# Three table rows taken out of the first loads, their spacing made 4/3 slots, and a gate step placed earlier on ScalarE

## The reference

```python
c_act = silu(c)
mod = c_act @ mod_w[l] + mod_b[l]                  # 6 vectors of 1024: sh1, sc1, g1, sh2, sc2, g2
h = rmsnorm(x, norm_g[l, 0]) * (1 + sc1) + sh1
proj = h @ w_in; q, k, v, og, gl = split(proj)
log_a = log_sigmoid(gl @ w_g2 + b_g2) / 16
b = cumsum(log_a)                                  # within chunks of 64 tokens
q_t = q * exp(b); k_t = k * exp(-b); k_dec = k * exp(b_last - b)
o = ...                                            # scores, values and a state carried over 4 chunks
x = x + g1 * ((rmsnorm(o, norm_g) * silu(og)) @ w_out)
cos, sin = rope_tables(positions)                  # needed much later, in the second block
```

## Time and profile before

| what | us |
|---|---|
| median of 3 runs | 3123.09 |
| lowest and highest | 3121.48, 3126.27 |
| profiled execution, its own time | 3126.55 |
| its span, first to last instruction | 3124.7 |
| first 16 modulation rows and norm, until TensorE starts slot 16 | 53.19 |
| slots 16 to 40 | 94.7 |
| from there to the start of slot 41 | 34.1 |

### The profile page before, as it was taken

One profiled execution on the slowest core, in us unless ns is written; L12 is line 12 of the kernel. 1 busy time (PEld: TensorE's weight loads), 2 busy tenths in 40 slices (PEclk: granted clock), 3 DMA queues, 4 the chain that ended last, 5 costly groups with the idle time before them and its releaser, 6 DMA issues.

```text
span 3124.7 us, 58935 instructions
## 1 busy us (share of the span) xinstructions
PE 2964.2 (95%) x18896; PEld 2681.5 (86%) x18896; DVE 2061.9 (66%) x3764; ACT 1578.5 (51%) x3099; POOL 1338.2 (43%) x1069
## 2 busy tenths in 40 slices
PE   7999999988999988999999799999899999999998
PEld 6679999987787777899999677878898889999997
DVE  6647953368888866389213988888653447777776
ACT  1225554577455555355555964555564235555554
POOL 5823988886544410069888844444000010000100
PEclk8999999999999997999999999999999999999998
DMA  6534557722766631445567046665354235555553
GB/s 248 206 105 153 182 194 263 262 106 76 260 229 225 221 120 55 138 158 183 180 214 259 0 179 249 226 221 206 129 179 139 95 128 193 191 194 197 193 192 124
DMA packets 153463, 552.58 MB, mean 177 GB/s; under 512 B 16896, under 2 KB 19712, under 8 KB 153232
## 3 DMA queue, kind: packets, MB, share of 16 engines
q1 hardware_dynamic: 151136, 547.42, 51.3%
q10 hardware_dynamic: 2224, 3.87, 0.4%
HBM read 550.17 MB, written 1.05 MB: 176 GB/s over the span
## 4 chain that ended last, share of the span: by engine, by line
PE 79%; ACT 8%; DVE 5%; issue 5%; POOL 3%; DMA 1%; ACTq 0%; DVEq 0%; POOLq 0%; SPq 0%
PE bank L983 20%; PE bank L1013 20%; PE bank L1256 12%; PE bank L724 7%; PE bank L776 7%; PE bank L1277 6%; ACT hT L1485 3%; POOL w_parts L2580 2%; PE bank L748 1%; ACT hT L1481 1%; PE bank L678 1%; ACT h_parts L1493 1%; DVE a_parts L2216 1%; DVE h_parts L2213 1%; ACT h_parts L1491 1%
## 5 line engine op out<-in xcount | busy, mean ns | idle before, releaser
L2580 POOL TENSOR_TENSOR w_parts<-ring,w_parts 128x512 fp32r<-128x512 f32 x512 | 659.3, 1307 | 423.4 <-ACT w_parts L1445 400.6
L983 PE MATMUL bank<-h_parts,w_parts 128*128 128x256 f32 x6144 | 750.1, 284 | 6.0 <-ACT arena L1381 4.4
L983 PEld LDWEIGHTS bank<-h_parts,w_parts 128*128 128x128 f32 x6144 | 741.7, 192 | 6.8 <-issue 4.8
L1445 ACT ACTIVATE w_parts<-ring 128x512 fp32r<-128x512 f32 x512 | 319.5, 631 | 342.6 <-PE bank L983 241.7
L1256 PEld LDWEIGHTS bank<-h_parts,w_parts 128*128 128x128 f32 x3072 | 374.5, 193 | 3.9 <-DVE arena L2442 1.5
L1256 PE MATMUL bank<-h_parts,w_parts 128*128 128x256 f32 x3072 | 375.4, 284 | 1.4 <-DVE arena L2442 1.4
L1643 ACT ACTIVATE w_parts<-ring 128x512 fp32r<-128x512 f32 x384 | 242.2, 632 | 266.2 <-PE bank L1256 166.1
L1013 PE MATMUL bank<-h_parts,a_parts 128*128 128x512 f32 x1536 | 366.4, 394 | 8.3 <-DVE a_parts L2216 8.3
L1013 PE MATMUL bank<-w_parts,a_parts 128*128 128x512 f32 x1536 | 371.6, 398 | 0.6 <-DVE a_parts L2216 0.6
L2511 DVE TENSOR_TENSOR w_parts<-ring,w_parts 128x512 fp32r<-128x512 f32 x376 | 271.0, 732 | 148.9 <-ACT w_parts L1643 145.7
L1013 PEld LDWEIGHTS bank<-h_parts,a_parts 128*128 128x128 f32 x1536 | 284.3, 188 | 84.5 <-DVE a_parts L2216 26.4
(11 more groups left out here) (345 smaller groups left out, 4492.2 us busy)
## 6 DMA issues: line engine op xcount, KB each, us to landing
ring<-stream SPq DMA_DIRECT2D x786, 512.0 KB, 3.4
arena<-stream SPq DMA_DIRECT2D x144, 512.0 KB, 4.3
hT<-stream SPq DMA_DIRECT2D x80, 512.0 KB, 4.5
mean<-stream SPq DMA_DIRECT2D x32, 512.0 KB, 4.5
arena<-consts ACTq DMA_DIRECT2D x1, 1536.0 KB, 6.6
xT<-xin ACTq DMA_DIRECT2D x1, 1024.0 KB, 10.8
out<-hT SPq DMA_DIRECT2D x4, 256.0 KB, 2.2
arena<-subk ACTq DMA_DIRECT2D x2, 128.0 KB, 2.1
```

The lines of the kernel that those rows point to most:

```text
L983: mm = pe.matmul(bank[k][:, 0:T], w[:, wp, ws], h_parts[:, hp, 4 * j + q, :], start=(j == 0 and q == 0 and i == 0), stop=(j == 1 and q == ...
L1445: act.activation(w_parts[half % HALVES][:, 0, :], ring[slot_][:, j * 512:(j + 1) * 512], ACT.Copy).then_inc(sem(f"{n}_high"), 1)
L2580: pool.tensor_tensor(w[:, 1, :], ring[(base + k) % RING][:, j * 512:(j + 1) * 512], w[:, 0, :].bitcast(F32), ALU.subtract).then_inc(sem(f" ...
```

## The change

The list `at` begins at slot 17 in place of slot 8, has 20 entries spaced by 4/3 slots in place of 14 spaced by 3/2, and leaves four in place of six behind slot 43. ScalarE's sigmoid and logarithm stand behind the eviction of the first key tile instead of the fourth.

```diff
             gla = MO["gla_gl"][0]
-            at = [8, 10, 14, gla + 1] + [gla + 2 + 3 * i // 2 for i in range(14)] + [gla + 27] * 6
+            at = [gla + 1 + 4 * i // 3 for i in range(20)] + [gla + 27] * 4
             loads_with_mods(0, MO["peer0_q"][1], MODS_GLA, MODS_GLA[0], at)
...
             for h in range(GH):
                 copy_act(act, G.q[:, h, :], f"g_q{h}")
-            for h in range(GH):
-                copy_act(act, G.k[:, h, :], f"g_k{h}")
-
+            copy_act(act, G.k[:, 0, :], "g_k0")
             act.wait_ge(sem("g_abs"), 1)
             act.activation(G.e, G.e, ACT.Sigmoid, scale=-1.0).then_inc(signal("g_act"), 1)
             act.wait_ge(sem("g_act"), signalled("g_act"))
             act.activation(G.e, G.e, ACT.Ln).then_inc(signal("g_ln"), 1)
             act.wait_ge(sem("g_ln"), signalled("g_ln"))
+            for h in range(1, GH):
+                copy_act(act, G.k[:, h, :], f"g_k{h}")
```

## The result

The changed kernel takes 3137.73 us, median of 20 runs (3119.06 to 3149.29), against 3124.44 (3114.95 to 3131.55, 20 runs) for the kernel before, measured with it: ratio 1.0038, 95% interval 1.0023 to 1.0052. It is slower, by 13 us, where 5 were forecast; 3137.73 lies above the range of 3117 to 3133.

A forecast was written before the change was run, and what follows sets the result against it. It took VectorE's first rows, then TensorE, with POOL's table rows just beginning to bind, as the bound. The 8.7 us won was nearly all lost to the rope, and late POOL rows made slot 40 5 later: 3123.1 + 5 = 3128, range 3117 to 3133.

The forecast's parts named there:

- Part 1: Start of the kernel: with rows moved out of the first loads, slot 16 starts at about 44.5, 8.7 us earlier.
- and still do: Start of the kernel: TensorE's last two direct rows run 31.45 to 38.44 as before, their loads waiting for the same readers.
- Part 2: VectorE's rope beside busy POOL: done at 65.3, slot 20 stalls 6.4; of the 8.7 us won, 0.6 is left.
- Part 3: POOL's table rows fall behind: row 6 starts at 82.9, so rows 6 to 15 must be made from there on.
- Part 4: Gate step three slots earlier: no gain itself; its chain costs POOL 16.6 us, all ahead of row 15, 2.8 previously behind it.
- The sum: Row 15 made at 144.5, slot 40 ends at 153 against 147.85, slot 41 due at 187: 5 us later, 3128.
- rival (b): Start's gain kept, POOL makes its 16 rows by 131: 3115 us; against it, rows need 88 and 82 are there; chance 0.12.
- 34.1 us of mostly TensorE work lead to 181.99: Stretch from slot 40's end at 147.85 to TensorE's start on slot 41, read from the profile before.
- Rival (c): No gap in POOL's first rows: rope ends at 68, late slots bring a second low-clock spell; 3132 us; chance 0.25.

The follow-up runs named there:

- e3: The changed kernel with ScalarE's two sines moved behind the key evictions and VectorE's sign product behind the gate chain; 3130.56 us, ratio 1.002.
- e2: The changed kernel with the old list of places put back, so only the gate's step is moved early; 3123.75 us, ratio 1.0004.
- e1: The kernel before with only the new list of places, the gate step left where it was; 3131.13 us, ratio 1.0029.
- e6: The kernel before with 30 tiny logarithms on ScalarE ahead of the head norms' logarithms, to make slot 41 late; 3129.64 us, ratio 1.001.
- a5: The changed kernel, unaltered, one profiled run; 3130.72 us at a clock of 0.974.
- a4: The changed kernel, unaltered, one profiled run; 3144.53 us at a clock of 0.969.
- a1: The changed kernel, unaltered, run again; 3129.19 us over 12 runs, ratio 1.0027.
- x3: The changed kernel with the table rows behind slots 38 and 39 moved to slot 41; 3139.93 us over 6 runs, ratio 1.005.
- z1: x3 with VectorE's two output-gate scalings moved behind the first four state copies; 3129.13 us over 9 runs, ratio 1.0027.
- e7: The changed kernel with late sines, respaced table rows and the last modulation group taken behind slots 41 to 48; 3123.64 us, ratio 0.9994.
- z2: e7 with VectorE's two output-gate scalings moved behind the first four state copies; 3108.48 us over 6 runs, ratio 0.9962.
- x2: e7, unaltered, one profiled run; 3119.53 us.
- x4: The kernel before with three table rows put behind slot 39, so that slot 40 waits long; 3140.91 us over 6 runs, ratio 1.0047.

## Why the prediction was wrong, point by point

- **Part 1 held, the gain is larger.** Slot 16 starts at 41.93, forecast 44.5. The last two direct rows run from 29.05 instead of 31.45, 2.4 of the 2.6: "and still do" was wrong. The load they wait for is issued 0.4 earlier (25.74 against 26.16) and lands after 3.3 instead of 5.3. It no longer has POOL's rows beside it on the queue, which is the likely reason; no run tests it. The gain is worth nothing, as the rope takes it.
- **Part 2 held.** The rope begins at 43.90 (46.4) and ends at 64.27 (65.3), 1.07 an operation, slot 20 starts at 65.78 (66.7) behind 7.91 (6.4). e3 shows that this wait is the reason: with the sines out of the way slot 41 is 8 earlier in the profile.
- **Part 3 held.** Row 6 starts at 82.23 (82.9).
- **Part 4: the price on POOL held, its cause in the move didn't.** Rows 6 to 15 take 82.23 to 143.65, 61.4, so the chain costs 16.4 beside ten rows of 4.5 (forecast 16.6, of which 0.86 was a wait of POOL for a load, at 102.25 in before). But that the move itself costs 2.8 was not borne out: e2 has row 15 only 1.1 later and slot 41 not later at all. With the new list the chain lies ahead of row 15's end at either place, since POOL is late there: e1, with the gate late, needs the same 61.4 for rows 6 to 15.
- **The sum held for the lower heap.** Row 15 is made at 143.65 (144.5), slot 40 ends at 152.5 (153), slot 41 starts at 186.63 (187). The lower heap's median is 5.2 over before, inside the range, and e6 shows that a slot 41 as late as this costs 4.7. One figure of rival (b), "82 are there", doesn't follow from its own numbers: from 43.8 to 131 are 87.2.
- **The term that failed is "34.1 us of mostly TensorE work lead to 181.99".** It was taken as a constant behind slot 40, and what POOL does there was costed only by its last row. It measured 34.1 again in the profiles of after (152.5 to 186.63) and a5, and 47.6 in a4 (151.9 to 199.51), which has the spell. The step that makes the difference had a row of its own in the trace of before, L1970 at 1.88 beside a POOL that had just paused. After the change POOL pauses at most 1.5 near there instead of 7.2, and in which of its four operations the scalings fall depends on when its last loads land. Where they fall on the product and first fold they take 3.1 to 3.7, TensorE waits half a microsecond or more, and in part of the runs its clock then goes to 1.2 GHz for most of the stage: 14 us. Eleven of the 20 runs lie in the upper heap, so the median stands there. How many do varies: a1, the same kernel, had 4 of 12 and a median of 3129.19, inside the range. So it is partly chance that the median of 20 came out at 3137.73. None of the rivals had this. Rival (c) had a second spell of low clock, but behind the stalls of the late slots, at 1.7 apiece.

Shown: the spell costs 14.0 (a4 against a5); it comes without a late stall (x3); with the wait taken away it is gone from the trace, and the clock is higher in each run, in the kernel whose runs all had a low clock (x3 against z1), and the upper heap of e7 is empty (z2). Not shown: the upper heap of after has one trace, a4; its other runs are known by their time and clock alone, and x2 shows that these don't settle it. Why a wait of 0.5 to 0.6 goes with the spell in two profiles of six is open, and so are e3's runs at 3130 to 3134, the three runs of e1 over 3140 and the one of e2: their kernels' profiles have no wait, but each is of a faster run. The edit of z1 on the changed kernel as it stands was not tried; by z1 one would expect it to leave the lower heap alone, some 5 over before.

## What to carry to other kernels

When work is shifted in time on one engine, look not only at who waits for it, but at which operations of another engine it now meets, above all ahead of a stage that TensorE runs alone with narrow products: in this kernel a wait of half a microsecond there went with a loss of 14 in some runs. An operation that nobody needs yet should not stand ahead of one that TensorE waits for. And when the runs of a kernel fall into two heaps, take traces until there is one of each, and compare those.

## What the runs showed of the hardware

- TensorE's granted clock fell to 0.50 in the state stage in four profiles, each with a wait of TensorE of 0.50 to 1.07 us ahead. In x2, x3 and x4 it fell within half a microsecond of the wait's end, in a4 2.6 behind it. It stayed there for 27 us in a4 (163.5 to 190.8) and 34 in x3 (157.0 to 191.2), although the engine was busy 5.00 of each 5 us. The products in it were of 64 columns, with groups of eight of 256 columns in between; such a group (L893) took 3.78 instead of 1.99. In each the clock rose again only while TensorE ran the 16 products of 256 columns behind them (L900).
- The same wait doesn't always go with it: 0.49 (twice), 0.55 and 0.63 brought no spell; 0.50, 0.54, 0.87 and 1.07 did.
- Two scalings of 128x1024 on VectorE take 1.6 (a1) to 3.7 us (x3, z1), by what POOL runs beside them.
- VectorE's 19 rope operations took 20.4 us beside a busy POOL (after) and 10.0 where POOL paused for most of them (before).
- With three loads of 512 KB fewer among the first 16, the load that TensorE's last two direct rows wait for landed after 3.3 us instead of 5.3.
